# The context's projection weights in wider, shorter pieces

## The chip, the cores and the metric

The kernel runs on one core of a Trainium2 chip. The metric is the device time of one execution in microseconds. Three executions of the kernel before took 1667.81, 1668.27 and 1671.95 us, so the median is 1668.27 us.

## The reference, cut to what matters

Two transformer blocks follow each other on 256 tokens of width 1024, all in 32-bit floats. The first block ends in a mixture of 32 experts; the second mixes tokens with two state-space scans, which start from states computed on a context of another 256 tokens. The context needs nothing of the first block, so its work can run beside the experts.

```python
def _hierarchical_moe(h, ...):                 # first block, 32 experts, 2 per token
    ...
    a = xb @ w_gate[ex]                        # 1024 x 512 per expert
    u = xb @ w_up[ex]                          # 1024 x 512
    y = (silu(a) * u) @ w_down[ex]             # 512 x 1024
...
def project(h, conv):                          # second block, for context and for latent tokens
    z, xbc, dt_raw, qkv, gate, b_raw, a_raw = split(h @ w_in, splits)
    xbc = silu(conv(xbc, conv_w_ssd) + conv_b_ssd)
    qkv = silu(conv(qkv, conv_w_gdn))
    ...
pc = project(h_ctx, dwconv)                    # the context: of xbc and qkv, 26 tiles of 128 columns are needed
pl = project(h_lat, conv_grid)
```

Here `h_ctx` is 256 x 1024 and each of the context's 26 channel tiles ("channels" below) is one product of a 1024 x 128 slice of `w_in` with the transposed context.

## The kernel before, in words

The program has four stages: the first block up to its router (to about 420 us), the mixed stage (to about 950 us), in which the experts and the context's work alternate, the second block's latent side, and its feed-forward part.

In the mixed stage each engine runs two generators of phases, `experts_...` and `context_...`, in one fixed order, `SCHEDULE`, that `mixed_schedule` (L158) writes from estimated costs. The part of it that matters here is, with e for an expert: `gate_up_a 0`, channel 2's slot, `gate_up_b 0`, channel 3, `turn 0`, `gate_up_a 1`, `gate_up_b 1`, channels 4 and 5, `down 0`, and so on. Channels 0 to 2 are multiplied before the stage, the others in pairs, about one pair per expert, up to channels 24 and 25 behind `down 11`. The phase `channelN` of TensorE is channel N's product (L740, 16 matmul records of L2120) and the transposes of channel N-2 (L2114). `gate_up_a e` and `gate_up_b e` are 32 records of L1915 each, `down e` 32 of L1937, `gather` 32 of L1899, `scatter` 8 of L1956, `ssd` the records of L637.

All weights come over one queue, that of SyncE (SP), in one order written out by `weight_stream` (L174). In the mixed stage it is a list of 205 pieces of 1 MiB: per expert two halves of the gate matrix (`ga`, `gb`), two of the up matrix (`ua`, `ub`) and two of the down matrix (`da`, `db`), each with runs of 4 or 8 KB in memory, and for the context `cx0` to `cx12`, one for two channels: 256 columns of all 1024 rows, in runs of 1 KB. A context piece stands in the list where its first channel stands in `SCHEDULE`, `cx0` and `cx1` at its head. The list begins

```
 0 cx0   1 cx1   2 ga0   3 ua0   4 gb0   5 ub0   6 ga1   7 ua1   8 gb1   9 ub1
10 cx2  11 da0  12 db0  13 ga2  14 ua2  15 gb2  16 ub2  17 cx3  18 da1  19 db1 ...
```

A piece lies in one slot. There are 8 slots in the ring and 5 lent by the area that other data use: places 11 and 12 until `ga9`, 8 and 9 until `ga12`, 10 until `ga20` (`LENT`, L26). So 13 slots serve up to `ga9`, 11 up to `ga12`, 9 from there to `ga20`. `unit_slot` (L501 to L517) gives each piece the slot that was given out longest ago (`oldest`, L494); it looks at the order in which slots were given out, not at when they come free. A gate and an up half take a pair from `PAIRS`.

SP goes through the list (L2912 to L2914): for each piece it first waits until the piece that held the slot before is done with (`wait_freed`, L522), and then issues the load. A wait holds back everything behind it in the list. A gate or up half is done with after its phase, a down half after its half of the phase, and a context piece after the product of its second channel:

```python
if n % 2:
    unit_freed[f"cx{n // 2}"] = filled, order.count
```

On the other side TensorE waits in `unit` (L2101) until the piece that it wants has landed. The names that the change touches are `weight_stream`, `unit_source` (which columns and rows a piece has, L441) and `context_channel_pe` (L740).

Of the kernel before, what the change touches and what calls it, by code (L numbers as in the profile page):

```python
# [14 lines left out]
P = 128  # L15
D = 1024
KD = D // P
SEQ = 256
# [9 lines left out]
WIDE = 512  # L28
# [142 lines left out]
    return order + [("context", phase) for phase, _ in context[taken:]]  # L171


def weight_stream(schedule):  # L174

    before = ["in0", "in1", "in2", "in3", "in4", "in9", "mk0", "mk1"]
    before += [f"in{i}" for i in (5, 6, 7, 8, 10, 11, 12, 13, 14, 15)]
    before += ["ad0", "ad1", "ad2", "ad3", "pc0", "pc1", "pa", "pm", "wo0", "wo1"]
    mixed = ["cx0", "cx1"]
    for stream, phase in schedule:  # L180
        kind, _, i = phase.partition(" ")
        if kind.startswith("gate_up"):
            mixed += [f"g{kind[-1]}{i}", f"u{kind[-1]}{i}"]
        if kind == "down":
            mixed += [f"da{i}", f"db{i}"]
        if kind.startswith("channel") and CTX_GAP <= int(kind[7:]) < 26:
            name = f"cx{int(kind[7:]) // 2}"
            if name not in mixed:
                mixed.append(name)
    mixed += [f"da{EXPERTS - 1}", f"db{EXPERTS - 1}"]  # L190
    after = ["xb0", "xb1", "xb2", "k0", "k1", "v0", "v1", "q0", "q1", "gt0", "gt1", "z0", "z1"]
    after += [f"ad{i}" for i in range(4, 12)] + [f"w2{i}" for i in range(4)]
    after += [f"{w}{i}" for i in range(6) for w in ("fg", "fu")] + [f"fd{i}" for i in range(6)]
    return before, mixed, after
# [5 lines left out]
def two_block_kernel(nc, a, out):  # L200

    before_experts, mixed_names, after_experts = weight_stream(SCHEDULE)
    ctx = ExitStack()
    with ctx:
# [3 lines left out]
        def sem(name):  # L208
            return ctx.enter_context(nc.semaphore(name))
# [196 lines left out]
        order = TileOrder()  # L406
        filled = sem("filled")
# [33 lines left out]
        def unit_source(name):  # L441

            kind, i = name.rstrip("0123456789"), int(name[len(name.rstrip("0123456789")):] or 0)
            if name.startswith("w2"):
                kind, i = "w2", int(name[2:])
            if kind in ("ga", "gb", "ua", "ub"):
                half = slice(4 * (kind[1] == "b"), 4 * (kind[1] == "b") + 4)
                return [(a["w_gate" if kind[0] == "g" else "w_up"][0, i].rearrange("(p k) n -> p k n", p=P)[:, half, :], 4)]
            if kind in ("da", "db"):
                first = 256 * (kind == "db")  # L450
                return [(a["w_down"][0, i, first:first + 256, :], 2)]
            if kind == "in":
                return [(a["w_in"][0, :, i * WIDE:(i + 1) * WIDE], 8)]
            if kind == "mk":
                return [(a["w_mem_kv"][0, :, i * WIDE:(i + 1) * WIDE], 8)]
            if kind == "pa":
                return [(a["w_proj_attn"][0], 2)]
            if kind == "pc":
                return [(a["w_proj_conv"][0, 512 * i:min(512 * i + 512, 768), :], 4 if i == 0 else 2)]
            if kind == "pm":  # L460
                return [(a["w_proj_mem"][0], 4)]
            if kind == "wo":
                return [(a["w_out"][0, :, i * WIDE:(i + 1) * WIDE], 8)]
            if kind == "ad":
                return [(a["w_ada_2"][0, :, i * WIDE:(i + 1) * WIDE], 8)]
            first = {"xb": 1024, "q": 2592, "k": 3616, "v": 4640, "z": 0, "gt": 5664}
            if kind in first:
                c = first[kind] + i * WIDE
                return [(a["w_in_2"][0, :, c:c + WIDE], 8)]
            if kind == "cx":  # L470
                c = 1024 + i * 256 if i < 5 else 3616 + (i - 5) * 256
                return [(a["w_in_2"][0, :, c:c + 256], 8)]
            if kind == "w2":
                return [(a["w_out_2"][0, 512 * i:512 * i + 512, :], 4)]
            if kind in ("fg", "fu"):
                w = a["w_ffn_gate_2" if kind == "fg" else "w_ffn_up_2"]
                return [(w[0, :, i * WIDE:min((i + 1) * WIDE, FFN)], 8)]
            assert kind == "fd", name
            return [(a["w_ffn_down_2"][0, 512 * i:min(512 * i + 512, FFN), :], 4 if i < 5 else 2)]
# [5 lines left out]
        def unit_views(name):  # L485

            views, (home, offset) = [], slot_place(unit_slot[name])
            for src, tiles in unit_source(name):
                width = src.shape[-1]
                views.append(home[:, offset:offset + tiles * width].rearrange("p (k n) -> p k n", k=tiles))  # L490
                offset += tiles * width
            return views
# [8 lines left out]
        for n, name in enumerate(stream, -len(before_experts)):  # L501
            if name not in mixed_names:
                slots = oldest([(slot, slot + 1) for slot in range(0, SLOTS if name in before_experts else KEPT, 2)])
            else:
                usable = [*range(SLOTS), *(slot for slot in LENT if n < mixed_names.index(LENT[slot][1]))]
                if name[0] == "g":
                    pair = oldest([pair for pair in PAIRS if pair[0] in usable and pair[1] in usable])
                if name[0] in "gu":
                    slots = pair[0:1] if name[0] == "g" else pair[1:2]
                else:  # L510
                    slots = oldest([(slot,) for slot in usable])
            unit_slot[name] = slots[0]
            held_before[name] = [holder[slot] for slot in slots if slot in holder]
            for slot in slots:
                holder[slot], taken_at[slot] = name, n
            arrivals[slots[0]] += 16 * len(unit_source(name))
            landed_by[name] = arrivals[slots[0]]  # L517
            if name == mixed_names[-1]:
                mixed_last = dict(holder)
        unit_freed = {}  # L520
# [218 lines left out]

        def context_channel_pe(pe, n, open_tile, unit, product):  # L740

            w, = unit(f"cx{n // 2}")
            product(open_tile(("channel", 0, n))[:, 0:SEQ], lambda k: w[:, k, n % 2 * P:(n % 2 + 1) * P],
                    lambda k: hB[0][:, k, :], KD).then_inc(filled, 1)
            if n % 2:
                unit_freed[f"cx{n // 2}"] = filled, order.count

        def context_pe(pe, open_tile, unit, transposes, product):

# [2139 lines left out]
        @block.sync  # L2889
        def _(sp):  # L2890
            def load(name):
                for dst, (src, tiles) in zip(unit_views(name), unit_source(name)):
                    rows = src if len(src.shape) == 3 else src.rearrange("(k p) n -> p k n", p=P)
                    sp.dma_start(dst, rows).then_inc(landed[unit_slot[name]], 16)

            for table, which in ((COLS_A, 0), (COLS_B, 1)):
                for name, (first, count) in table.items():
                    src = a[name]
                    flat = {1: "(a p) -> a p", 2: "x (a p) -> (x a) p", 3: "x y (a p) -> (x y a) p"}[len(src.shape)]
                    sp.dma_start(rows_a[first:first + count, which, :], src.rearrange(flat, p=P)).then_inc(s["rows_in"], 16)  # L2900
            sp.dma_start(rows_a[0:MOD_COLS, 2, :], a["b_ada_2"][0, 0:2 * D].rearrange("(a p) -> a p", p=P)).then_inc(s["rows_in"], 16)
            sp.wait_ge(s["x_in"], 16)
            for n, name in enumerate(before_experts):
                if n == 2:
                    sp.dma_start(mem, a["mem"][0].rearrange("(t p) d -> p t d", p=P)).then_inc(s["mem_in"], 16)
                wait_freed(sp, name)
                load(name)
            wait_filled(sp, ("values", 15))
            for first, c in ((0, 2560), (32, 6688)):
                sp.dma_start(dta_w[:, :, first:first + 32], a["w_in_2"][0, :, c:c + 32].rearrange("(k p) n -> p k n", p=P))\  # L2910
                  .then_inc(s["dta_in"], 16)
            for name in mixed_names:  # L2912
                wait_freed(sp, name)
                load(name)  # L2914
            where_overflow(sp, lambda: rest_sp(sp))
            second_block_sp(sp, load)
# [25 lines left out]
```

## Time and profile before

| | us |
|---|---|
| median of 3 executions | 1668.27 |
| the profiled execution, its own time | 1670.5 |
| its span in the profile | 1668.8 |
| busy: TensorE / VectorE / ScalarE / GpSimd | 1539.2 / 687.3 / 381.1 / 211.8 |
| loaded by the SP queue | 361.13 MB |

The times of the rows are microseconds from the start of the span. A matmul in 32 bits shows as two records, so one channel's product of 8 matmuls is `x16`. Where two operations follow each other on TensorE their records overlap a little, since the engine is pipelined. "idle before <-X" in brackets is how long an engine waited and for what. A DMA share of 1.0 in a stretch means that all 16 engines that move data were busy throughout (a little over 1 where their packets overlap). "us to landing" runs from the issue of a load on SP to the arrival of its last byte's signal. Of the instructions of SP only the issue is shown, and its duration includes the time in which the queue took nothing more; the wait before an issue is not shown as such.

### The profile page before, as it was taken

The page shows a single profiled execution, that of the slowest core. Times are in us where ns is not written, and L with a number is a line of the kernel's source. Part 1 is how long each engine was busy: PE and PEld are TensorE (multiplying, and loading weights), DVE is VectorE, ACT ScalarE, POOL GpSimd, SP SyncE. Part 2 cuts the span into 40 slices and gives each one's busy share as a digit, 9 for nine tenths or more (in the row PEclk, how much of TensorE's full clock was granted, in tenths as well). Part 3 has the DMA queues.
Part 4 walks back from the last instruction along what each step waited for, and adds up shares of the span by engine and source line. Part 5 has one row for each costly group of instructions (what it writes and reads, how often), then busy time and mean ns, then how long its engine had stood idle before and what let it go on. Part 6 is the DMA issues. An engine that isn't in the chain of part 4 may idle for free.

```text
span 1668.8 us, 22991 instructions
## 1 busy us (share of the span) xinstructions
PE 1539.2 (92%) x9387; PEld 1052.8 (63%) x9387; DVE 687.3 (41%) x1457; ACT 381.1 (23%) x846; POOL 211.8 (13%) x362
## 2 busy tenths in 40 slices
PE   7999999999899797888998899999989999999996
PEld 3548655555666464556676478865568854888742
DVE  2206311432544334634453357777877642200003
ACT  1001154321411112232332132143333410100000
POOL 2000000000000000133313000001545430200000
PEclk9999999999899899999999899999989999999998
DMA  9444422664599999999999923341333343343430
GB/s 310 158 151 152 151 101 101 227 210 162 204 407 407 407 406 412 367 417 417 415 412 417 384 88 133 134 150 53 119 144 121 133 149 124 132 152 126 176 126 25
DMA packets 124029, 370.43 MB, mean 222 GB/s; under 512 B 10507, under 2 KB 26517, under 8 KB 107413
## 3 DMA queue, kind: packets, MB, share of 16 engines
q1 hardware_dynamic: 118277, 361.13, 57.0%
q0 software_dynamic: 1280, 6.29, 1.0%
q10 hardware_dynamic: 4368, 1.54, 0.4%
q8 instruction: 76, 1.25, 0.3%
q14 instruction: 28, 0.23, 0.0%
HBM read 367.89 MB, written 1.05 MB: 221 GB/s over the span
## 4 chain that ended last, share of the span: by engine, by line
PE 75%; DMA 12%; DVE 7%; ACT 3%; issue 1%; SPq 0%; DVEq 0%; ACTq 0%
PE psum L2120 50%; PE psum L660 7%; DMA ring<-in_w_up 5%; PE psum L1915 4%; DMA ring<-in_w_down 4%; PE psum L2114 3%; DMA area<-in_w_down 2%; PE psum L1937 2%; PE psum L1899 2%; PE psum L1956 2%; PE psum L2268 1%; PE psum L2238 1%; PE psum L686 1%; PE psum L637 1%; PE psum L840 1%
## 5 line engine op out<-in xcount | busy, mean ns | idle before, releaser
L2120 PE MATMUL psum<-ring,area 128*128 128x512 f32 (+1 forms) x1040 | 449.9, 591 | 8.2 <-DMA ring<-in_w_in 2.6
L2120 PE MATMUL psum<-area,ring 128*128 128x256 f32 (+1 forms) x1824 | 390.1, 374 | 3.5 <-DMA ring<-in_w_in 1.8
L2120 PEld LDWEIGHTS psum<-area,ring 128*128 128x128 f32 x1824 | 335.1, 191 | 48.6 <-issue 2.5
L2120 PEld LDWEIGHTS psum<-ring,area 128*128 128x128 f32 x1040 | 197.4, 192 | 245.4 <-issue 243.0
L660 PEld LDWEIGHTS psum<-area 128*128 128x128 f32 x1216 | 145.1, 197 | 24.2 <-issue 15.5
L660 PE MATMUL psum<-area 128*128 128x128 f32 x1216 | 153.4, 284 | 7.3 <-DVE area L1366 6.0
L1915 PE MATMUL psum<-ring,area 128*32 128x256 f32 x1984 | 127.7, 405 | 28.7 <-DMA ring<-in_w_up 28.6
L2393 ACT ACTIVATE area<-psum 128x512 f32<-128x512 f32 x108 | 61.5, 598 | 393.2 <-PE psum L2120 330.7
L1915 PEld LDWEIGHTS psum<-ring,area 128*32 128x32 f32 x1984 | 65.4, 115 | 78.5 <-issue 46.1
L1266 DVE SCALAR_TENSOR_TENSOR area<-area,cols 128x268 f32<-128x268 f32 (+1 forms) x186 | 91.6, 492 | 6.6
L2114 PE MATMUL psum<-const,area 128*128 128x128 f32 x506 | 80.2, 285 | 14.1 <-ACT area L1040 4.1
L2114 PEld LDWEIGHTS psum<-const,area 128*128 128x128 f32 x506 | 62.7, 145 | 46.0 <-issue 24.2
L2120 PE MATMUL psum<-area 128*128 128x256 f32 (+3 forms) x384 | 79.6, 360 | 5.2 <-DVE area L1444 2.7
L2120 PEld LDWEIGHTS psum<-area 128*128 128x128 f32 (+1 forms) x384 | 64.0, 194 | 18.5 <-issue 6.0
L1662 POOL TENSOR_TENSOR area<-area 128x1024 f32<-128x1024 f32 x4 | 9.8, 2463 | 475.0 <-DVE area L2516 475.0
L1024 ACT COPY area<-psum 128x256 f32<-128x256 f32 x62 | 23.1, 373 | 189.4 <-PE psum L2120 189.4
L1652 DVE TENSOR_TENSOR area<-psum,area 128x512 f32<-128x512 f32 x11 | 7.6, 692 | 142.3 <-PE psum L2120 142.3
L1264 DVE TENSOR_SCALAR area<-area,cols 128x268 f32<-128x268 f32 (+1 forms) x62 | 22.1, 356 | 97.9 <-ACT area L1024 96.6
L1062 ACT COPY area<-psum 128x512 f32<-128x512 f32 x88 | 50.2, 590 | 45.7 <-PE psum L660 40.3
L1937 PE MATMUL psum<-ring,area 128*32 128x256 f32 x720 | 48.0, 397 | 11.7 <-DMA ring<-in_w_down 11.5
L1612 DVE TENSOR_TENSOR area<-psum,area 128x512 f32<-128x512 f32 x8 | 5.5, 687 | 117.8 <-PE psum L2120 117.8
L1713 POOL TENSOR_TENSOR area<-area 128x120 f32<-128x120 f32 (+14 forms) x120 | 43.9, 366 | 51.3 <-ACT area L1086 42.5
(337 smaller groups left out, 1461.2 us busy)
## 6 DMA issues: line engine op xcount, KB each, us to landing
ring<-in_w_gate SPq DMA_DIRECT2D x62, 1024.0 KB, 14.7
ring<-in_w_up SPq DMA_DIRECT2D x62, 1024.0 KB, 14.9
ring<-in_w_in SPq DMA_DIRECT2D x29, 2048.0 KB, 8.2
ring<-in_w_down SPq DMA_DIRECT2D x45, 1024.0 KB, 15.9
ring<-in_w_ada SPq DMA_DIRECT2D x12, 2048.0 KB, 8.0
area<-in_w_down SPq DMA_DIRECT2D x19, 1024.0 KB, 15.0
ring<-in_w_out SPq DMA_DIRECT2D x6, 2048.0 KB, 7.8
ring<-in_w_ffn_gate SPq DMA_DIRECT2D x5, 2048.0 KB, 7.8
```

The lines of the kernel that those rows point to most:

```text
L660: last = nc.tensor.matmul(dst[:, i * P:(i + 1) * P], lhs(4 * h + i), rhs(4 * h + i), start=True, stop=True)
L1024: nc.scalar.copy(dst, src).then_inc(drain_of(key), 1)
L1062: nc.scalar.copy(dst[:, 4 * h:4 * h + 4, :], src).then_inc(drain_of((key, m, h)), 1)
L1266: link(v.scalar_tensor_tensor(dst, src, w, dst, ALU.mult, ALU.add))
L1713: link(g.tensor_tensor(tmp[:, 0:n, :], rep[:, left, :, j], Y[:, j:j + 1, :].to_broadcast([P, n, GDN_HEADS]), ALU.mult))
L1899: last = nc.tensor.matmul(dst[:, j * P:(j + 1) * P], h2[:, t, k * P:(k + 1) * P], place[:, t, q * P:(q + 1) * P], start=t == 0, stop=t == ...
L1915: last = nc.tensor.matmul(wide.dst[CAP * j:CAP * (j + 1), 0:2 * P], hcT[:, q % 2, k, rows], both[:, :, k % 4, j * P:(j + 1) * P], start=k ...
L1937: last = nc.tensor.matmul(dst[CAP * g:CAP * (g + 1), 0:256], actT_e[:, e % 2, CAP * j:CAP * (j + 1)], w[:, j % 2, g * 256:(g + 1) * 256], ...
L1956: nc.tensor.matmul(dst, placeT[:, q, t * P:(t + 1) * P], y_quad[:, q % 2, half * WIDE:(half + 1) * WIDE], start=True, stop=True).then_inc( ...
L2114: last = nc.tensor.transpose(t[0:width, j * P:j * P + rows], src, ident[0:rows, 0:rows])
L2120: last = nc.tensor.matmul(dst, lhs(k), rhs(k), start=first and k == 0, stop=final and k == count - 1)
L2393: nc.scalar.activation(dst, src, func).then_inc(drain_of(key), 1)
```

## The change

Twenty-four of the 26 channels are loaded in groups of four, as two pieces: `cxaG` has rows 0 to 511 and `cxbG` rows 512 to 1023 of the group's 512 columns. A piece is 1 MiB as before, in runs of 2 KB. Channels 8 and 9 lie at the end of one block of columns and keep one piece of 256 columns, `cx2`. So there are 13 context pieces as before and 205 pieces in the list. A group's pieces stand where its first channel stands in `SCHEDULE`, the first group's at the head. Each channel's product takes its first four k tiles from one piece and its last four from the other, and both pieces are done with after the group's last channel. `SCHEDULE`, the slots and the rule that gives them out stay.

```diff
+CTX_GROUPS = ((0, 1, 2, 3), (4, 5, 6, 7), (8, 9), (10, 11, 12, 13), (14, 15, 16, 17), (18, 19, 20, 21), (22, 23, 24, 25))
+def context_units(n):
+    g, group = next((g, group) for g, group in enumerate(CTX_GROUPS) if n in group)
+    return [f"cxa{g}", f"cxb{g}"] if len(group) == 4 else [f"cx{g}"], group
...
-    mixed = ["cx0", "cx1"]
+    mixed = ["cxa0", "cxb0"]
...
-            name = f"cx{int(kind[7:]) // 2}"
-            if name not in mixed:
-                mixed.append(name)
+            mixed += [name for name in context_units(int(kind[7:]))[0] if name not in mixed]
...
-            if kind == "cx":
-                c = 1024 + i * 256 if i < 5 else 3616 + (i - 5) * 256
-                return [(a["w_in_2"][0, :, c:c + 256], 8)]
+            if kind in ("cx", "cxa", "cxb"):
+                c = 1024 + i * WIDE if i < 3 else 3616 + (i - 3) * WIDE
+                w = a["w_in_2"][0, :, c:c + (256 if kind == "cx" else WIDE)]
+                return [(w, 8)] if kind == "cx" else [(w[0:D // 2] if kind == "cxa" else w[D // 2:], 4)]
...
-            w, = unit(f"cx{n // 2}")
-            product(open_tile(("channel", 0, n))[:, 0:SEQ], lambda k: w[:, k, n % 2 * P:(n % 2 + 1) * P],
+            names, group = context_units(n)
+            parts = [unit(name)[0] for name in names]
+            tiles, at_group = KD // len(parts), n - group[0]
+            product(open_tile(("channel", 0, n))[:, 0:SEQ], lambda k: parts[k // tiles][:, k % tiles, at_group * P:(at_group + 1) * P],
                     lambda k: hB[0][:, k, :], KD).then_inc(filled, 1)
-            if n % 2:
-                unit_freed[f"cx{n // 2}"] = filled, order.count
+            if n == group[-1]:
+                for name in names:
+                    unit_freed[name] = filled, order.count
```

## Rows read from the trace of the kernel before

**Rows 1.** The page: DMA's busy tenths in 40 slices of 41.7 us.

```profile
DMA  9444422664599999999999923341333343343430
```

**Rows 2.** Windows: stretch, length, busy time by engine, TensorE's clock, DMA share, GB/s.

```profile
420.00:444.00 24.00, 20.56 (x156) 16.95 (x154) 14.72 (x48) 11.12 (x18) 0.00 (x0) 0.86 0.36 132
450.00:650.00 200.00, 177.15 (x1644) 123.83 (x1637) 74.89 (x172) 33.62 (x96) 0.00 (x0) 0.93 1.03 407
670.00:690.00 20.00, 20.00 (x183) 11.38 (x185) 16.13 (x27) 6.73 (x10) 4.20 (x2) 1.00 0.78 313
692.00:942.00 250.00, 219.84 (x2469) 155.44 (x2465) 104.31 (x226) 71.44 (x162) 68.03 (x148) 0.97 1.02 415
```

**Rows 3.** TensorE's longest waits, 444 to 960 us: total, times, longest.

```profile
PE psum L1915 <- DMA ring<-in_w_up: 28.6, 16, 4.1
PE psum L1937 <- DMA ring<-in_w_down: 11.5, 12, 1.5
```

**Rows 4.** Timeline of SP's issues, 419 to 455 us: start, duration, load.

```profile
419.57 0.38 SPq L2894 DMA_DIRECT2D ring<-in_w_in  x1
419.99 1.10 SPq L2894 DMA_DIRECT2D area<-in_w_down  x2
444.13 0.34 SPq L2894 DMA_DIRECT2D ring<-in_w_gate  x1
...
446.71 7.46 SPq L2894 DMA_DIRECT2D ring<-in_w_down  x2
```

**Rows 5.** DMA in 500:620, then issues in 444:444.3, and 1000:1600: KB, us to landing.

```profile
DMA packets 13700, 48.78 MB, mean 406 GB/s; under 512 B 739, under 2 KB 6939, under 8 KB 10117
...
ring<-in_w_gate SPq DMA_DIRECT2D x1, 1024.0 KB, 5.0
...
ring<-in_w_ffn_gate SPq DMA_DIRECT2D x5, 2048.0 KB, 7.8
...
ring<-in_w_ffn_down SPq DMA_DIRECT2D x4, 2048.0 KB, 7.6
```

**Rows 6.** Timeline of TensorE: channels 4, 7, 10, `down 4`'s second half, channel 13.

```profile
453.21 3.72 PE L2120 MATMUL psum<-area,ring 128*128 128x256 f32 x16
...
474.24 3.62 PE L2120 MATMUL psum<-area 128*128 128x256 f32 x16
...
502.37 6.53 PE L2120 MATMUL psum<-area 128*128 128x256 f32 x16 [1.67 <-DMA area<-in_w_in]
...
517.51 1.07 PE L1937 MATMUL psum<-area 128*32 128x256 f32 x16 [0.26 <-DMA area<-in_w_down]
...
525.92 3.62 PE L2120 MATMUL psum<-area 128*128 128x256 f32 x16
```

**Rows 7.** Timeline of TensorE: `gate_up_a 8`, channels 16 and 17, `gate_up_b 8`.

```profile
558.64 3.64 PE L1915 MATMUL psum<-ring,area 128*32 128x256 f32 x32 [3.83 <-DMA ring<-in_w_up]
...
566.22 3.62 PE L2120 MATMUL psum<-area 128*128 128x256 f32 x16
...
569.99 1.93 PE L1915 MATMUL psum<-ring,area 128*32 128x256 f32 x32
```

**Rows 8.** Timeline of TensorE: channel 18 and channel 21.

```profile
586.61 3.72 PE L2120 MATMUL psum<-area 128*128 128x256 f32 x16
...
609.34 3.62 PE L2120 MATMUL psum<-area 128*128 128x256 f32 x16
```

**Rows 9.** Timeline of TensorE: `down 11`'s second half to channel 25, and `ssd0`.

```profile
642.34 1.07 PE L1937 MATMUL psum<-ring,area 128*32 128x256 f32 x16 [0.56 <-DMA ring<-in_w_down]
645.22 3.72 PE L2120 MATMUL psum<-area,ring 128*128 128x256 f32 x16 [1.81 <-DMA ring<-in_w_in]
...
649.00 3.62 PE L2120 MATMUL psum<-area,ring 128*128 128x256 f32 x16
...
662.57 0.55 PE L2114 MATMUL psum<-const,area 128*128 128x128 f32 x3 [0.86 <-ACT area L1040]
665.27 3.58 PE L637 MATMUL psum<-area 128*128 128x512 f32 x4 [2.15 <-DVE area L1419]
```

## The prediction, made before the change was run

> **What bounds the kernel now.** I began with the page. TensorE is busy 92% of the span, which tells little; of the slices, DMA's are at 9 only at the start and in slices 11 to 22, about 460 to 950 us [rows 1]. That is the mixed stage. The windows say how full it is there: a DMA share of 1.03 at 407 GB/s in 450 to 650 us and 1.02 at 415 GB/s in 692 to 942, with one hole between (0.78 in 670 to 690, some 4.3 us of idle engines) [rows 2]. The view of TensorE's waits agrees: in this stage it waits for up and down matrices 40.1 us in all [rows 3]. So from 450 to 945 us time is bytes over rate, and whatever leaves the DMA engines idle in that stretch is paid in full. Before it the engines are two thirds idle: 132 GB/s in 420 to 444 us [rows 2].
>
> The timeline of SP tells why. At 419.6 us it issues `cx2`, `da0` and `db0`, places 10 to 12 of the list, then nothing until 444.13 [rows 4], when the list's next piece, `ga2`, gets its place: it is `cx1`'s, and that is free after channel 3. The three pieces are 3.15 MB; 132 GB/s over 24 us is 3.17 MB. They are moved in time that would be idle.
>
> **The change part by part.** TensorE's products keep their count, order and shape; the second wait in each channel is for a piece that landed with the first, within one piece's time. I cost both at nothing: TensorE's 40.1 us of waiting cover them. The head of the list, now `cxa0` and `cxb0`, is loaded well before 420 us as before. SP issues 205 loads as before. What changes is the runs, and who waits for whom.
>
> *Runs.* At 415 GB/s a piece takes 2.53 us. The 500 to 620 us view has 48.78 MB, which at that rate is 117.5 us, so 2.5 us are the price of its pieces in 1 KB runs: (6939 - 739) packets of 1 KB, 6.05 pieces, so 0.41 us each [rows 5]. A 2 MiB load in 2 KB runs lands in 7.8 us on an idle queue, one in 4 KB runs in 7.6 [rows 5], so 2 KB runs cost about 0.1 us a MiB. Ten context pieces follow 444 us at 0.41 before; after it is ten at 0.1 and `cx2` at 0.41: 4.1 less 1.4 saves 2.7 us, between 0 and 4.
>
> The Trainium skill, "DMA: Bandwidth & Descriptors", Specifications, gives 512 bytes as the smallest transfer for line rate; by it 1 KB runs cost nothing and the saving is zero. The 407 against 415 GB/s does not agree, so the row stands.
>
> *Slots.* I applied the slot rule of L494 to L517 to the new list. A piece waits for the former holder of its slot, and all behind it on SP's queue waits too. Before, a context piece was free after its second channel, soon after its landing; now it is held through four channels, about an expert longer, and the rule, which goes by the order of giving out, still gives its slot away 12 or 13 pieces later (9 or 10 at the end, where fewer slots are left). Six loads now wait for the end of a group. The last column counts pieces that are issued already and are needed only later, the cover of the DMA engines during the wait:
>
> | place, load | waits for | cover |
> |---|---|---|
> | 10 `cxa1` | channel 3 (`cxa0`) | the idle time of before |
> | 22 `gb3` | channel 7 (`cxa1`) | 4 |
> | 46 `db5` | channel 13 (`cxa3`) | 5 |
> | 60 `db7` | channel 17 (`cxa4`) | 3 |
> | 76 `ua11` | channel 21 (`cxa5`) | 5 |
> | 89 `ga13` | channel 25 (`cxb6`) | 0 |
>
> Before, the smallest cover up to there was 5, mostly 8 to 12, and the engines had no hole until 670 us.
>
> *The start.* `cxa1` at place 10 waits for channel 3, until 444.1 us, and with it `cxb1`, `da0` and `db0`. So 195 pieces follow 444 us, not 192: 3 x 2.53 = 7.6 us. Less the 2.7 of the runs: **+4.9 us**. Channel 4, at 453.2 us [rows 6], is not late: `cxb1` lands about 444.1 + 5.0 + 2.6 = 451.7.
>
> *The stops.* A load on an idle queue lands 5.0 us after its issue [rows 5], and SP issues 0.1 us after release, so a stopped load lands 5.1 us after its channel ends. Undisturbed it would land 2.53 us after the piece ahead of it. I take TensorE's way to the channel's end from the rows, from the landing it waits for:
> - Channel 7 ends at 474.24 + 3.62 = 477.9 [rows 6], unmoved. `gb3` lands at 483.0. Undisturbed: `cxa1` lands at 449.2, and 12 pieces later it is 479.5. Stop 3.5 us.
> - From the landing of `db4` (place 40, 517.5) to the end of channel 13 (529.5) [rows 6] are 12.0 us. 12.0 + 5.1 - 6 x 2.53 = 1.9 us.
> - From `ua8` (place 56, 558.6) to the end of channel 17 (569.8) [rows 7] are 11.2 us, with `gate_up_a 8` at 3.64 us, the 1.2 GHz level; at 2.4 GHz, 1.93 as in the last of those rows, 9.5. 11.2 or 9.5 + 5.1 - 4 x 2.53: 6.2 or 4.5. I take the middle, 5.4 us.
> - Channels 18 and 19 wait for `cxb5` (place 66), so the way runs from the start of channel 18 (586.6) to the end of channel 21 (613.0) [rows 8], 26.4 us with no DMA wait in it. 26.4 + 5.1 - 10 x 2.53 = 6.2 us.
> - `down 11`'s second half takes 1.07 us from the landing of `db11` (place 88), channels 24 and 25 take 649.00 + 3.62 - 645.22 = 7.4 [rows 9]. 8.5 + 5.1 - 2.53 = 11.1 us, with nothing in flight.
>
> Sum **+28.1 us**. The bounds: 1.5 less at the first stop if the queue fills slower after 444, 0.9 either way at channel 17, and upward more of the 1.2 GHz level.
>
> [...]
>
> *Given back.* Behind channel 25 TensorE waits 0.86 us for ScalarE and 2.15 for VectorE before `ssd0` [rows 9]. With `ga13` to `db12` about 10 us later relative to channel 25, both are ready by then. TensorE so reaches `gate_up_a 14`, which frees the place that ends the hole at 670 to 690, 3.0 us sooner after `db12`: **-3.0 us**, between 0 and the hole's 4.3. From 692 us on the queue has no hole and the list's order and places are the same but for slot numbers, so what DMA has lost by then comes out at the end; the latent side starts from the last down piece and nothing there runs on a clock of its own.
>
> *Sum.* 4.9 + 28.1 - 3.0 = +30.0 us. The profiled execution's span 1668.8 becomes 1698.8, its own time 1670.5 becomes 1700.5; that execution lies 2.2 us above the median 1668.27, which becomes **1698 us**.
>
> **Rivals.**
> - *Runs decide (faster).* Ten pieces save up to 4 us and the stops are covered by what is queued: 1664 us. For it: SP's issue takes 7.46 us at 446.7 [rows 4], so the queue was full with places free, and DMA stays at 1.03 until 650. Against: a cover of 0 to 5 pieces is 0 to 13 us of work, TensorE's ways are 8.5 to 26. It decides only if channel 25 ends before `db11` has landed, and that TensorE goes through `down 11` first excludes this unless the order on chip differs.
> - *Only the start and channel 25.* The four middle stops vanish because TensorE is not waiting where I start its ways, or the engines keep queued packets longer than I count: 4.9 + 11.1 - 3.0 = +13, 1681 us. For it: the full queue again. Against: at 517, 558 and 642 the rows show TensorE waiting for the very piece.
> - *The clock too.* Longer waits put TensorE at the 1.2 GHz level: channel 10, behind a wait, took 6.53 us, not 3.62 [rows 6]. If channels 12, 18 and 24 go that way, 2.9 us each, and `gate_up_a 10` (1.7) with them, the stops grow by 10: 1708 us. For it: the clock is 0.93 in 450 to 650 already [rows 2]. Against: 3.72 at channel 24 behind a wait of 1.81 us [rows 9].
> - *It does not do what it says.* If runs of 2 KB cost what 1 KB does, 2.7 us are not saved: 1701, inside the forecast's range.
>
> **How the numbers follow.** Forecast 0.66, with 1690 to 1704 from its bounds; start and channel 25 alone 0.14; the clock 0.13; faster 0.04; no change 0.03, as a mix of covers nobody sees here. To leave no more than 2 in 10 out, the range takes in the second and the third: 1681 to 1709. A measurement tells 0.3% (5 us) from no change. Faster 0.04, same 0.03, slower 0.93.
>
> **What would show it.** In the profile after: SP issues nothing at 419 us, and the DMA share of 420 to 444 falls to nearly none; `cxa1` to `db0` follow 444. TensorE's waits for DMA grow from 40 to some 65 us, with the longest, about 7 us, at `gate_up_a 13`. The DMA share in 10 us windows dips below 1 at five places, the deepest behind channel 25, and the 1 KB packets nearly vanish. From `gate_up_a 17` on everything is the same, late by the same 30 us. If the share stays at 1.03 through 450 to 670, the stops are wrong; if `cxa1` issues before channel 3 ends, the start is.

## The result, and the profile after

The changed kernel takes 1707.19 us, the median of 4 executions from 1702.93 to 1710.62, beside 1668.52 us for the kernel before. The ratio is 1.0221 with a 95% interval from 1.0193 to 1.025: 32 to 42 us slower. The profiled execution took 1705.28 us, its span is 1703.5 us against 1668.8, so the trace has 34.7 us to explain. The prediction was 1698 us, +30 us, in a range from 1681 to 1709.

In the changed kernel the phases have other line numbers: a channel's product is L2131, gate and up L1926, down L1948, transposes L2125, `ssd` L645, and SP's loads L2905.

The page's DMA slices of the kernel after answer to [rows 1]. Where slices 12 to 23 were all 9, slices 14, 15 and 16 (554 to 681 us) are now 8, 8 and 7:

```profile
DMA  9444424553599887999999943332152334344430
```

The windows of the kernel after have the same columns as [rows 2]. From 735 us on the rate of before is there. Ahead of that are one empty stretch at the start and five new holes; the dip at 710 to 720 us is the hole that the kernel before had at 670 to 690 [rows 2].

```profile
420.00:444.00 24.00, 19.38 (x156) 15.50 (x154) 15.89 (x49) 12.30 (x21) 0.00 (x0) 0.93 0.02 2
450.00:470.00 20.00, 18.85 (x176) 14.58 (x173) 7.37 (x17) 4.62 (x11) 0.00 (x0) 1.00 1.02 417
470.00:480.00 10.00, 10.00 (x96) 7.12 (x94) 5.97 (x14) 2.55 (x7) 0.00 (x0) 1.00 0.77 296
530.00:550.00 20.00, 18.80 (x159) 13.62 (x161) 9.17 (x20) 2.85 (x8) 0.00 (x0) 1.00 0.89 341
570.00:590.00 20.00, 15.29 (x132) 10.26 (x132) 5.57 (x14) 1.65 (x5) 0.00 (x0) 0.83 0.64 251
620.00:640.00 20.00, 18.07 (x172) 11.59 (x170) 9.31 (x20) 2.64 (x8) 0.00 (x0) 1.00 0.68 269
660.00:680.00 20.00, 12.38 (x114) 8.77 (x105) 6.12 (x15) 2.53 (x8) 0.00 (x0) 0.99 0.44 167
710.00:720.00 10.00, 10.00 (x91) 4.41 (x93) 8.90 (x15) 0.28 (x1) 2.79 (x2) 1.00 0.70 270
735.00:970.00 235.00, 211.58 (x2364) 150.91 (x2368) 97.19 (x206) 66.75 (x151) 68.24 (x148) 0.98 1.02 415
```

The timeline of SP's issues of the kernel after shows what ends each hole: a load that follows a long silence. The `cxa1` group, which [rows 4] had in part at 419.57, comes at 442.41; then `gb3` at 475.93, `db5` at 540.54, `ua11` at 632.10 and `ga13` at 677.06. (`db7` stands in the merged line at 557.60; SP's next load is 584.57.)

```profile
442.41 0.38 SPq L2905 DMA_DIRECT2D ring<-in_w_in  x1
...
475.93 0.33 SPq L2905 DMA_DIRECT2D ring<-in_w_gate  x1
...
540.54 0.38 SPq L2905 DMA_DIRECT2D area<-in_w_down  x1
...
557.60 26.92 SPq L2905 DMA_DIRECT2D area<-in_w_down  x2
584.57 0.47 SPq L2905 DMA_DIRECT2D area<-in_w_gate  x1
...
632.10 0.34 SPq L2905 DMA_DIRECT2D ring<-in_w_up  x1
...
677.06 0.34 SPq L2905 DMA_DIRECT2D ring<-in_w_gate  x1
```

The timeline of TensorE of the kernel after gives the other end of each: channel 7's last product ends at 474.00 + 1.89 = 475.9, channel 13's at 540.5, channel 17's at 584.1, channel 21's at 632.1, channel 25's at 677.0. Each of the five loads is issued within 0.1 us of it, or in `db7`'s case at the end of the line that covers it.

```profile
474.00 1.89 PE L2131 MATMUL psum<-area 128*128 128x256 f32 x8
...
513.47 6.50 PE L2131 MATMUL psum<-area 128*128 128x256 f32 x16 [4.04 <-issue]
...
536.89 3.62 PE L2131 MATMUL psum<-area 128*128 128x256 f32 x16
...
572.73 3.64 PE L1926 MATMUL psum<-ring,area 128*32 128x256 f32 x32 [3.71 <-DMA ring<-in_w_up]
...
582.22 1.89 PE L2131 MATMUL psum<-area,ring 128*128 128x256 f32 x8
...
595.40 3.64 PE L1926 MATMUL psum<-area 128*32 128x256 f32 x32 [5.03 <-DMA area<-in_w_up]
...
630.18 1.89 PE L2131 MATMUL psum<-area 128*128 128x256 f32 x8
...
668.63 1.07 PE L1948 MATMUL psum<-ring,area 128*32 128x256 f32 x16 [1.32 <-DMA ring<-in_w_down]
...
675.14 1.89 PE L2131 MATMUL psum<-area,ring 128*128 128x256 f32 x8
...
684.78 3.64 PE L1926 MATMUL psum<-ring,area 128*32 128x256 f32 x32 [7.42 <-DMA ring<-in_w_up]
...
694.77 1.07 PE L1948 MATMUL psum<-ring,area 128*32 128x256 f32 x16 [0.53 <-DMA ring<-in_w_down]
...
979.11 1.94 PE L1948 MATMUL psum<-ring,area 128*32 128x256 f32 x16 [0.58 <-DMA ring<-in_w_down]
```

Three lines of the same view of the kernel before, not shown ahead, are needed beside them:

```profile
578.03 3.64 PE L1915 MATMUL psum<-ring,area 128*32 128x256 f32 x32 [4.12 <-DMA ring<-in_w_up]
...
660.27 1.07 PE L1937 MATMUL psum<-ring,area 128*32 128x256 f32 x16 [1.38 <-DMA ring<-in_w_down]
...
944.17 1.94 PE L1937 MATMUL psum<-ring,area 128*32 128x256 f32 x16 [0.55 <-DMA ring<-in_w_down]
```

At places where TensorE waits for the queue in both kernels, the delay can be read like a stopwatch. (At channel 10 the row of the kernel after names "issue", but `cxb3`, its second piece, landed at 513.4 us, just before the product began.) Where the changed list has one piece more ahead of the one waited for, its 2.5 us are taken off before the difference to the place before is formed (us):

| TensorE reaches | before | after | late by | less one piece | lost since | predicted |
|---|---|---|---|---|---|---|
| channel 10 (start, and stop behind channel 7) | 502.4 | 513.5 | 11.1 | 8.6 | 8.6 | 4.9 + 3.5 |
| `gate_up_a 8` (channel 13) | 558.6 | 572.7 | 14.1 | 11.6 | 3.0 | 1.9 |
| `gate_up_a 9` (channel 17) | 578.0 | 595.4 | 17.4 | 17.4 | 5.8 | 5.4 |
| `down 11`, second half (channel 21) | 642.3 | 668.6 | 26.3 | 23.8 | 6.4 | 6.2 |
| `down 12`, second half (channel 25) | 660.3 | 694.8 | 34.5 | 34.5 | 10.7 | 11.1 |
| the last down piece | 944.2 | 979.1 | 34.9 | 34.9 | 0.4 | -3.0 |

Of the signs that the prediction named, the empty start, the five dips with the deepest behind channel 25, and the longest wait at `gate_up_a 13` (7.42 us, put at about 7) are there. TensorE's waits for DMA from 444 us to the end of the stage are 46.7 us before and 67.2 after, besides 8.3 at channels whose rows name "issue".

### The profile page after: what moved, and what is told of

Its sections match the earlier page's. It is cut to its first block, busy times and chain, and to the rows that moved or that the text cites. A ratio compares the mean times of both kernels' runs of the same rounds, so it can differ in the third digit from the quotient of the medians.

```text
span 1703.5 us, 22991 instructions
## 1 busy us (share of the span) xinstructions
PE 1545.8 (91%) x9387; PEld 1054.7 (62%) x9387; DVE 687.6 (40%) x1457; ACT 380.7 (22%) x846; POOL 212.0 (12%) x362
## 4 chain that ended last, share of the span: by engine, by line
PE 73%; DMA 15%; DVE 7%; ACT 3%; issue 2%; SPq 1%; ACTq 0%; DVEq 0%
PE psum L2131 50%; PE psum L668 7%; DMA ring<-in_w_down 7%; DMA ring<-in_w_up 6%; PE psum L1926 4%; PE psum L2125 3%; PE psum L1967 2%; PE psum L1910 1%; PE psum L1948 1%; PE psum L2279 1%; PE psum L2249 1%; DMA area<-in_w_in 1%; PE psum L694 1%; PE psum L645 1%; PE psum L851 1%
## 5 line engine op out<-in xcount | busy, mean ns | idle before, releaser
L2131 PE MATMUL psum<-ring,area 128*128 128x512 f32 (+1 forms) x1040 | 449.4, 591 | 7.3 <-DVE area L1389 2.1
L2131 PE MATMUL psum<-area,ring 128*128 128x256 f32 (+1 forms) x1824 | 391.4, 374 | 3.9 <-issue 2.3
L2131 PEld LDWEIGHTS psum<-area,ring 128*128 128x128 f32 x1824 | 335.1, 191 | 49.9 <-issue 6.0
L2131 PEld LDWEIGHTS psum<-ring,area 128*128 128x128 f32 x1040 | 197.2, 192 | 244.4 <-issue 242.1
L1926 PE MATMUL psum<-ring,area 128*32 128x256 f32 x1856 | 121.3, 408 | 44.1 <-DMA ring<-in_w_up 43.9
L1926 PEld LDWEIGHTS psum<-ring,area 128*32 128x32 f32 x1856 | 62.1, 115 | 91.7 <-issue 63.0
L2131 PE MATMUL psum<-area 128*128 128x256 f32 (+3 forms) x384 | 83.7, 368 | 12.0 <-issue 6.0
L2125 PE MATMUL psum<-const,area 128*128 128x128 f32 x506 | 80.3, 285 | 14.1 <-ACT area L1051 4.1
L2125 PEld LDWEIGHTS psum<-const,area 128*128 128x128 f32 x506 | 62.7, 145 | 45.9 <-issue 24.6
L2131 PEld LDWEIGHTS psum<-area 128*128 128x128 f32 (+1 forms) x384 | 66.1, 199 | 25.8 <-issue 13.5
L1948 PE MATMUL psum<-ring,area 128*32 128x256 f32 x800 | 52.6, 392 | 12.2 <-DMA ring<-in_w_down 11.9
L2081 DVE TENSOR_TENSOR area<-psum,area 128x128 f32<-128x128 f32 x32 | 9.3, 290 | 112.4 <-ACT area L2033 112.4
## 6 DMA issues: line engine op xcount, KB each, us to landing
area<-in_w_down SPq DMA_DIRECT2D x14, 1024.0 KB, 11.6
```

Of the source, the lines that this page charges most:

```text
L1926: last = nc.tensor.matmul(wide.dst[CAP * j:CAP * (j + 1), 0:2 * P], hcT[:, q % 2, k, rows], both[:, :, k % 4, j * P:(j + 1) * P], start=k ...
L1948: last = nc.tensor.matmul(dst[CAP * g:CAP * (g + 1), 0:256], actT_e[:, e % 2, CAP * j:CAP * (j + 1)], w[:, j % 2, g * 256:(g + 1) * 256], ...
L2125: last = nc.tensor.transpose(t[0:width, j * P:j * P + rows], src, ident[0:rows, 0:rows])
L2131: last = nc.tensor.matmul(dst, lhs(k), rhs(k), start=first and k == 0, stop=final and k == count - 1)
```

## The experiments

The times of different comparisons are set against their own runs of the kernel before, whose medians were 1670.23, 1670.62 and 1670.48 us in the three.

**Other slots, same pieces.** The slot rule alone is changed: a slot counts as old by the phase in which its holder is done with, not by when it was given out.

```diff
+        def released(name):
+            kind, i = name.rstrip("0123456789"), name[len(name.rstrip("0123456789")):]
+            if kind[:2] == "cx":
+                last = CTX_GROUPS[int(i)][-1]
+                return phases.index(f"channel{last}") + 0.5 if last >= CTX_GAP else 0.5
+            if kind in ("da", "db"):
+                phase = f"down {i}" if f"down {i}" in phases else "end"
+                return phases.index(phase) + (0.4 if kind == "da" else 0.8)
+            return phases.index(f"gate_up_{kind[1]} {i}") + 0.5
...
-                holder[slot], taken_at[slot] = name, n
+                holder[slot], taken_at[slot] = name, 1 + released(name) / 2 if name in mixed_names else n
```

> The changed kernel, its wide pieces and its list as they are; only the slot rule differs: a piece gets the slot whose holder is done with first in TensorE's order of phases, not the one given out longest ago. Theory (slots held through four channels and given away too early cause the loss): no load waits for the end of a group with less than 5 pieces of cover, so the five stops (28 us) go; cxa1, cxb1 and da0 take the lent slots at 419 us and db0 waits for gate_up_a 0 at 437 us and not for channel 3 at 444, so 195 - 3 pieces follow 437 us: 6.5 us earlier than in the kernel before, and 2.7 us are saved by the 2 KB runs. About 1660 us, 47 below the changed kernel and 8 below the kernel before. Rival (it is the pieces themselves that cost: two waits and two tiles in each product, an order of the list in which a whole group stands ahead of expert weights): the slots change little, 1695 to 1707 us.

Measured: 1661.83 us, 0.9949 of the kernel before (0.9934 to 0.9963), 45 us below the changed kernel. The same windows of this kernel, where the changed kernel had 0.77, 0.89, 0.64, 0.68 and 0.44:

```profile
470.00:480.00 10.00, 10.00 (x93) 7.41 (x96) 5.64 (x13) 2.55 (x7) 0.00 (x0) 1.00 1.04 399
530.00:550.00 20.00, 19.02 (x227) 12.59 (x231) 8.46 (x19) 2.92 (x9) 0.00 (x0) 1.00 1.03 415
570.00:590.00 20.00, 14.72 (x104) 10.32 (x107) 3.35 (x8) 1.69 (x7) 0.00 (x0) 0.83 1.03 409
620.00:640.00 20.00, 16.13 (x162) 10.22 (x161) 7.25 (x17) 3.37 (x10) 0.00 (x0) 0.91 1.02 418
660.00:680.00 20.00, 20.00 (x165) 11.71 (x164) 15.38 (x24) 5.22 (x9) 4.20 (x2) 0.99 0.80 316
```

The five holes are gone, with the same pieces in the same order; the 0.80 in the last window is the hole of before, which comes earlier in this kernel (`ssd0` at 656.88 us, not 665.27). So the loss is not that of the pieces themselves or of their order: the rival is out. The start moved as expected, only earlier still: SP's timeline has both `cx` pieces at 404.66 and the next load after them at 437.63, so the queue goes on 6.5 us before the kernel before's 444.13. These 6.5 us, the 7.6 us of three pieces loaded ahead of that, and the some 31 us of holes worked out below make the 45 us.

```profile
404.66 1.06 SPq L2918 DMA_DIRECT2D area<-in_w_in  x2
410.43 1.13 SPq L2918 DMA_DIRECT2D area<-in_w_down  x1
437.63 0.37 SPq L2918 DMA_DIRECT2D ring<-in_w_down  x1
```

**The same rule for the kernel before.** The edit is the one above on the kernel before, with `last = 2 * int(i) + 1`.

> The kernel before, with its narrow pieces, and the same slot rule as in release_order: the slot whose holder is done with first. Theory: its covers were 5 pieces or more already, so nothing changes but the start: ga2 also loads at 419 us and the queue goes on at 437 us, not 444, with 191 pieces left, 9 us earlier in all: about 1660 us. Against release_order this shows what the width of the pieces is worth once the slots are right: the runs save 2.7 us there, one more piece at the start saves 2.5 here, so the two should be within 2 us. Rival (width itself costs): this one is well ahead of release_order, by 25 us or more.

Measured: 1664.31 us, 0.9965 (0.9952 to 0.9977). The rule gives 6 us (4 to 8) to the kernel before, where 9 were expected; the rest stays open. It gives 45 to the changed one, so nearly all of the changed kernel's loss was the old rule's meeting with long-lived pieces. Wide and narrow are then 2.5 us apart, wide ahead, with intervals that overlap.

**Narrow pieces, held by fours.** Width is taken out, list and slots stay:

```diff
...
+    group = next(group for group in CTX_GROUPS if n in group)
+    return list(dict.fromkeys(f"cx{m // 2}" for m in group)), group
...
+            mixed += [name for name in context_units(int(kind[7:]))[0] if name not in mixed]
...
-            if n % 2:
-                unit_freed[f"cx{n // 2}"] = filled, order.count
+            names, group = context_units(n)
+            if n == group[-1]:
+                for name in names:
+                    unit_freed[name] = filled, order.count
```

> The kernel before with its narrow pieces of 256 columns for two channels in 1 KB runs, each product from one piece as before; but the two pieces of a group of four channels stand together in the list where the group's first channel stands, and both are given back after the group's last channel. So list and slots are those of the changed kernel, without its width, its two-piece products and its second waits. Theory: the loss is there in full, and the 2 KB runs' saving is missing: 1705 to 1712 us. Rival (width, two waits): about the kernel before, 1668 us.

Measured: 1708.54 us, 1.0236 (1.0217 to 1.0254). The loss is there without wide pieces, two-tile products or second waits. The runs' saving of 2.7 us can't be told here; the ratios of this and the changed kernel overlap.

**The start alone.** In the kernel before `cx0` is given back later:

```diff
-            if n % 2:
+            if n % 2 and n > 1:
                 unit_freed[f"cx{n // 2}"] = filled, order.count
+            if n == 3:
+                unit_freed["cx0"] = filled, order.count
```

> The kernel before with one edit: cx0 is given back after channel 3 and not after channel 1. The load of cx2, and da0 and db0 behind it, so waits until 444 us as cxa1 does in the changed kernel; nothing else moves. Theory: three pieces of 2.53 us more follow 444 us in a stretch that is bound by the DMA engines, +7.6 us: 1676 us. Rival (DMA has slack to catch up with them behind 444 us, since TensorE waits for DMA first at 498 us): 1668 us.

Measured: 1678.44 us, 1.0048 (1.0032 to 1.0063), so +8.2 us by the medians, 5.3 to 10.5 by the interval, where 7.6 was expected. SP's timeline has the load that stood at 419.57 [rows 4] behind channel 3:

```profile
443.75 0.38 SPq L2896 DMA_DIRECT2D ring<-in_w_in  x1
444.18 1.09 SPq L2896 DMA_DIRECT2D area<-in_w_down  x2
```

DMA does not catch up: three pieces moved out of an idle stretch into a full one cost about their own time.

**The last group alone.** The kernel before with wide pieces for channels 22 to 25; groups of two stand for the rest, and a group's columns follow from its first channel.

```diff
+CTX_GROUPS = ((0, 1), (2, 3), ..., (20, 21), (22, 23, 24, 25))
...
+    mixed = ["cx0", "cx1"]
...
+                n = CTX_GROUPS[i][0]
+                c = 1024 + n * P if n < 10 else 3616 + (n - 10) * P
```

> The kernel before, with wide pieces for the last group alone (channels 22 to 25); channels 0 to 21 keep their narrow pieces for two channels, and the slot rule is that of before. Theory: one stop is left, ua13 (place 90) waits for channel 25 with one piece of cover. TensorE's way of 8.5 us from db11's landing, 5.1 us to land, less 2 x 2.53: 8.5 us, less 0.6 for two pieces in 2 KB runs: +8 us, about 1678 us; the DMA share dips once, behind channel 25. TensorE's waits of 0.86 us for ScalarE and 2.15 us for VectorE before ssd0 stay, because VectorE turns to that work only after down 12, and so nothing is given back. Rival (they were to shrink to nothing when TensorE comes later): +5 us and the two waits gone. Rival (the stops cost only when they follow each other): 1670 us.

Measured: 1678.86 us, 1.0058 (1.0039 to 1.0078): +8.2 us, as expected; the interval, 6.5 to 13 us, leaves out the 5 and the 0 us of the rivals. TensorE's timeline of this kernel shows the stop behind channel 25 as a wait of 4.92 us at `gate_up_a 13`, and ahead of `ssd0` the two waits of [rows 9] as they were:

```profile
657.92 3.64 PE L1927 MATMUL psum<-ring,area 128*32 128x256 f32 x32 [4.92 <-DMA ring<-in_w_up]
...
668.85 1.07 PE L1949 MATMUL psum<-ring,area 128*32 128x256 f32 x16 [1.32 <-DMA ring<-in_w_down]
...
671.15 0.55 PE L2126 MATMUL psum<-const,area 128*128 128x128 f32 x3 [0.86 <-ACT area L1052]
673.85 3.49 PE L646 MATMUL psum<-area 128*128 128x512 f32 x4 [2.15 <-DVE area L1431]
```

So one stop is paid by itself, and nothing of it is given back.

**All but the last group.** The changed kernel with `(22, 23), (24, 25)` at the end of `CTX_GROUPS` and the same columns.

> The changed kernel, but channels 22 to 25 have narrow pieces for two channels as before. Theory: the stop behind channel 25 (11.1 us) goes and the four others and the start stay: 1707 - 11 = 1696 us, with dips of the DMA share behind channels 7, 13, 17 and 21 and none behind channel 25. Rival (the loss is that of the longer list ahead of the experts in all groups, evenly): a sixth of it goes, 1701 us.

Measured: 1694.06 us, 1.0159 (1.0136 to 1.0182). Against the changed kernel's 1.0221 that is 0.0062 of 1670 us, 10.4 us less, where the stop was priced at 11.1. The two intervals leave 4 to 16 us, so the time alone does not exclude the rival's 6; the windows do. They have the four earlier holes as they were and the last one filled:

```profile
470.00:480.00 10.00, 10.00 (x81) 7.61 (x77) 4.59 (x11) 2.04 (x6) 0.00 (x0) 1.00 0.77 296
530.00:550.00 20.00, 18.80 (x149) 13.61 (x153) 9.27 (x19) 2.96 (x8) 0.00 (x0) 1.00 0.89 349
570.00:590.00 20.00, 14.50 (x117) 9.95 (x116) 6.23 (x15) 2.48 (x8) 0.00 (x0) 0.83 0.65 254
620.00:640.00 20.00, 18.72 (x173) 12.38 (x175) 9.76 (x20) 2.65 (x8) 0.00 (x0) 1.00 0.67 263
660.00:680.00 20.00, 14.70 (x101) 10.05 (x101) 3.86 (x9) 1.77 (x6) 0.00 (x0) 0.83 1.03 405
```

**The runs alone.** Narrow pieces held by fours with the new slot rule, beside a second run of the first experiment. The edits are those above, put together.

> The kernel narrow_held (pieces of 256 columns in 1 KB runs, issued and held by fours) with the slot rule of release_order, so list and slots are those of release_order and only the runs differ, 1 KB and not 2 KB, with one tile and one wait in a product. Theory (1 KB runs cost 0.41 us a piece, 2 KB runs 0.1): ten pieces follow the start of the full stretch, so this is 2 to 3 us slower than release_order in the same comparison, and its data rate in 470 to 660 us is 407 GB/s, not 412. Rival (runs of 512 bytes or more are all at full rate, so that the price read from the windows is something else): the same time and the same rate.

> release_order once more, in the same comparison as narrow_release, so that the two are read against the same runs of the kernel before: 0.995 of the kernel before, 1661 us.

Measured: 1662.79 us, 0.9963 (0.9945 to 0.998), and 1660.70 us, 0.9946 (0.9927 to 0.9965). The medians differ by 2.1 us the expected way, but the intervals overlap, so the time alone does not settle it. The rate speaks for it: the windows 470 to 660 us, narrow first, then wide, both with full engines, one profile each. In the same window the kernel before and the one with its slot rule changed, narrow too, have 407 GB/s, and the first run of the wide kernel with the new slot rule 412.

```profile
470.00:660.00 190.00, 161.89 (x1531) 111.33 (x1529) 74.93 (x171) 32.79 (x108) 0.00 (x0) 0.94 1.03 405
```

```profile
470.00:660.00 190.00, 164.95 (x1543) 114.43 (x1542) 77.25 (x174) 35.05 (x122) 0.00 (x0) 0.94 1.02 411
```

## Why the prediction was right, and where it was not

*The bound.* From 450 to 945 us time was bytes over rate; each hole in the DMA share reached the end. Between `down 12` and the last down piece the delay grew by 0.4 us only.

*The start.* Three pieces more behind channel 3 were put at 7.6 us; alone they cost 8.2 (5.3 to 10.5). In the profiled execution channel 3 ended 1.7 us earlier than before (442.41 against 444.13 us), which the forecast had left unmoved. The change does not seem to do that: with the same list and slots up to there, the load behind channel 3 was issued at 444.18 us in the trace of the narrow pieces held by fours and at 444.02 in that of all but the last group. It is luck of this execution, and it hides part of an error in the next term.

*The stops.* The slot rule, applied on paper to the new list, named the five loads, and the timeline has each of them issued as its channel ends. Their sum was put at 28.1 us. In the table the stops stand less what the runs save on the way, and the first row has the earlier channel 3 in it, so its 8.6 for 8.4 agrees better than its parts. The DMA share shows them bare: what the five windows lack to 1.02 is 2.5, 2.6, 7.6, 6.8 and 11.6 us, 31 in all, where 3.5, 1.9, 5.4, 6.2 and 11.1 were forecast. This is the second error, of size alone: the sum was 3 us short, most of it behind channel 17. There the forecast took the middle between two clocks, but `gate_up_a 8`, which lies on that way, ran at the 1.2 GHz level again (granted clock 0.50, 3.64 us), which prices the stop at 6.2; the rest is not explained. With 31 for the stops, 7.6 - 1.7 - 2.7 + 31 is 34.2 us, beside 34.5 at `down 12`. The least cover made the dearest stop, and the two experiments on the last group put it at 8.2 us with one piece of cover (8 expected) and 10.4 with none (11.1).

The Trainium skill, "DMA: Bandwidth & Descriptors", Anatomy of one DMA, a section on loads issued from GpSimd, says that a semaphore wait happens on the issuing sequencer, while the DMA engines only work off their queues. The trace agrees for SP's loads: the DMA share falls to 0.44 in 660 to 680 us while SP stands at `ga13`, though by 661 us the next three pieces behind it had free slots.

*Given back.* This is the step whose reason failed. "Both are ready by then" put -3.0 us on TensorE's waits ahead of `ssd0`, and they are 0.86 and 2.15 us after as before; in the ten profiles of this document they lie from 0.59 to 0.86 and from 2.05 to 2.16:

```profile
697.07 0.55 PE L2125 MATMUL psum<-const,area 128*128 128x128 f32 x3 [0.86 <-ACT area L1051]
699.77 3.53 PE L645 MATMUL psum<-area 128*128 128x512 f32 x4 [2.15 <-DVE area L1430]
```

VectorE's timeline of the kernel after tells why. The work that `ssd0` waits for (L1430) stands in VectorE's order behind the copies out of `down 12` (L2059, L2061), so it begins after that phase however late the phase is; ScalarE's L1051 too begins, at 696.61 us, behind ScalarE's own copies out of `down 12`.

```profile
695.98 0.42 DVE L2059 COPY area<-psum 32x256 f32<-32x256 f32 x1 [1.83 <-PE psum L1948]
696.74 0.42 DVE L2061 COPY area<-psum 32x256 f32<-32x256 f32 x1 [0.33 <-ACT area L2020]
697.19 0.78 DVE L1286 COPY area<-psum 128x256 f32<-128x256 f32 x2
...
698.49 1.23 DVE L1430 TENSOR_TENSOR area<-area 128x1024 f32<-128x1024 f32 x1
```

I had taken the releaser's line for an engine that runs by itself. The hole of before came again, at 710 to 720 us, with some 3 us of idle engines for some 4.5; nothing of that shows in the delay, which grew by 0.4 us. Without this term the sum was 4.9 + 28.1 = 33.0; with the stops' 3 us and the 0.4, less channel 3's 1.7, it is the 34.7 measured between the spans. So the total came out nearer than its terms.

*The runs.* Priced at 2.7 us for ten pieces; 405 against 411 GB/s over 190 us is 2.8 us. The Trainium skill, "DMA: Bandwidth & Descriptors", Specifications, names 512 bytes as the least for line rate; these rates do not agree, 1 KB runs move less than 2 KB runs with the engines as full. In the medians of the narrow and the wide kernel with the new slot rule it is 2.1 us, not told from noise.

*The rivals.* That the runs decide is out, and so is that only the start and channel 25 count: the three stops between channel 7's and channel 25's are 15.2 us in the table. "The clock too" named 1708 us, nearest to the median of 1707.19, but not for its reason: of the four phases that it named, channels 12, 18 and 24 took 3.6 to 3.7 us and `gate_up_a 10` 1.93, all at 2.4 GHz (granted clock 1.00). Channels 8 and 10 ran mostly at the 1.2 GHz level (6.50 us at 513.47, granted clock 0.56), but they lie on no stop's way. The channels whose end releases a stopped load ran at 2.4 GHz, 3.6 us each. On a stop's way the lower level came at `gate_up_a 8`, as in the kernel before, and at the start of channel 16 behind it.

*What stays open.* The medians are 38.7 us apart and the profiled spans 34.7, for the profiled execution after lies 1.9 us below its median and that of before 2.0 above its own. Channel 3's 1.7 us would make up most of the first; whether it does is not shown. The changed kernel's four executions lie 7.7 us apart, those of before 4.1. No run here tells why.

## What to carry to other kernels

Before pieces are made to live longer, write out for every load whose release it waits for and how many pieces are issued already that are needed only after that release; where these pieces and the stopped one, each at a piece's time, take less than the consumer's way to the release and a load's time to landing, a queue in order has a hole of about the difference. Here a ring that gives out slots in the order of allotting cost 6 us while lives were short and 45 when some grew long; ordered by release, the same wide pieces went from 1.0221 to 0.9949 of the kernel before. And a wait that seems to offer something back has to be followed to what its releaser itself waits for.

## What the runs showed of the hardware

A load of 1 MiB on an idle queue took 5.0 us from issue to landing at 444.13 and at 681.22 us in the kernel before, and 4.9 to 5.4 us where a load ended a silence in the kernel after; the stops priced with 5.0 came out within 2.2 us each. With full engines the rate went with the runs: 405 to 407 GB/s where about one piece in seven has 1 KB runs, 411 to 412 with 2 KB in their place, and 415 in the later stretch that has 4 and 8 KB alone.
